# The RWKV scan of a four-layer network: the factors of the inverse applied one by one, products laid crosswise

## The reference

```python
def step(S, inp):
    rt, wt, kt, vt, kkt, bt = inp
    sk = jnp.einsum('bhij,bhj->bhi', S, kkt)
    S = S * wt[:, :, None, :] - sk[..., None] * bt[:, :, None, :] + vt[..., None] * kt[:, :, None, :]
    return S, jnp.einsum('bhij,bhj->bhi', S, rt)
S, ys = lax.scan(step, S0, xs, reverse=reverse)
```

## Time and profile before

| | us |
|---|---|
| median of three runs (2982.25 to 2987.36) | 2986.35 |
| the profiled execution | 2984.68 |
| its span in the trace | 2982.9 |
| PE busy | 2852.2 |
| DVE busy | 2072.6 |
| ACT busy | 604.3 |
| POOL busy | 306.7 |

### The profile page before, as it was taken

The page is one execution under the profiler, slowest core; times in us unless marked ns, Lnnn a source line. Parts: engine busy times, 40 slices in busy tenths (PEclk is TensorE's granted clock), DMA queues, the critical chain, the costliest instruction groups (busy, mean ns, idle before and its releaser), DMA issues.

```text
span 2982.9 us, 62866 instructions
## 1 busy us (share of the span) xinstructions
PE 2852.2 (96%) x27428; PEld 2641.3 (89%) x27428; DVE 2072.6 (69%) x3617; ACT 604.3 (20%) x1385; POOL 306.7 (10%) x518
## 2 busy tenths in 40 slices
PE   7999998889989999999999999989999999999998
PEld 6888886777887999999899999977889999977998
DVE  6777636555564798997869889836249989853864
ACT  2000004343332200201320021024121021022201
POOL 0001002432341001001000100000000100000000
PEclk8999999999999999999999999999999999999999
DMA  7556413003103688687347868733457868823452
GB/s 282 169 177 233 139 46 110 3 4 113 46 4 127 204 269 279 214 280 241 99 159 259 298 205 268 239 108 117 138 181 249 297 206 260 278 75 99 142 191 92
DMA packets 387504, 514.54 MB, mean 172 GB/s; under 512 B 14032, under 2 KB 344976, under 8 KB 386080
## 3 DMA queue, kind: packets, MB, share of 16 engines
q1 hardware_dynamic: 347632, 366.73, 37.9%
q0 software_dynamic: 39456, 143.67, 14.0%
q10 hardware_dynamic: 144, 0.13, 0.0%
HBM read 509.44 MB, written 1.05 MB: 171 GB/s over the span
## 4 chain that ended last, share of the span: by engine, by line
PE 87%; DVE 5%; ACT 3%; DMA 2%; issue 2%; POOL 1%; SPq 0%; DVEq 0%; ACTq 0%; POOLq 0%
PE PS L2580 39%; PE PS L2640 20%; PE PS L662 6%; PE PS L682 5%; PE PS L839 3%; PE PS L1754 2%; PE PS L1679 2%; PE PS L2652 1%; PE PS L1530 1%; PE PS L2500 1%; PE PS L1436 1%; PE PS L698 1%; PE PS L2518 1%; DMA W<-in_ffn_in 1%; DMA W<-in_e_w_in 0%
## 5 line engine op out<-in xcount | busy, mean ns | idle before, releaser
L2580 PE MATMUL PS<-X,W 128*128 128x128 f32 x3360 | 411.9, 276 | 6.2 <-ACT JUNK L2763 3.3
L2580 PEld LDWEIGHTS PS<-X,W 128*128 128x128 f32 x3360 | 393.2, 192 | 7.9 <-ACT JUNK L2763 4.8
L2640 PE MATMUL PS<-ARENA,W 128*128 128x128 f32 (+1 forms) x2816 | 362.3, 288 | 2.6 <-DVE ARENA L2943 1.6
L2640 PEld LDWEIGHTS PS<-ARENA,W 128*128 128x128 f32 x2816 | 346.3, 192 | 12.6 <-DVE ARENA L2943 2.0
L2867 DVE SCALAR_TENSOR_TENSOR ADAW<-ADAW,CB 128x1024 f32<-128x1024 f32 x280 | 332.4, 1218 | 0.6
L2471 POOL DMA_DIRECT2D ADAW<-in_ada_rows x272 | 144.4, 532 | 1820.8 <-DVE ADAW L2867 1476.4
L2580 PE MATMUL PS<-Y,W 128*128 128x128 f32 (+2 forms) x2096 | 311.8, 302 | 2.8 <-DVE Y L3178 1.8
L2580 PEld LDWEIGHTS PS<-Y,W 128*128 128x128 f32 x2096 | 285.2, 192 | 18.6 <-issue 1.8
L2580 PE MATMUL PS<-Y,ARENA 128*128 128x128 f32 (+2 forms) x1632 | 217.1, 286 | 2.2 <-DVE ARENA L2928 2.2
L2580 PEld LDWEIGHTS PS<-Y,ARENA 128*128 128x128 f32 x1632 | 203.1, 191 | 7.5 <-DVE ARENA L2928 3.0
L2914 DVE TENSOR_TENSOR ARENA<-W 128x1024 f32<-128x1024 f32 (+1 forms) x120 | 159.3, 1327 | 16.7 <-DMA W<-in_ffn_in 5.7
(11 more groups left out here) (470 smaller groups left out, 4313.2 us busy)
## 6 DMA issues: line engine op xcount, KB each, us to landing
...
```

Of the source, the lines that this page charges most:

```text
L2580: last = mm(block_bank(b, q, half), w[left][:, k, q * P:(q + 1) * P], yb[right][:, k], start=(k == 0 and p not in (2, 5)), stop=(k == 3), ...
L2640: last = mm(block_bank(b, 0, half), w[left][:, k], hb[right][:, k], start=(k == 0 and p not in (2, 5)), stop=(k == PAIRS - 1), skip_group_ ...
```

## The change

The inverse is no longer put together. DD and the factors (F, F2, F4 of MO x DD) are applied to the right side one by one: DG = DD x GG, then F4I, F2I and FI (U1, U2, UU). GG comes in two parts, GS from the state (copied by ACT) and GV from the values, added on DVE. The values have one form, VT1, UU0 and VT0 are gone. Scores, masks and most lists are laid out crosswise, by direction; N2 and M2 stay straight, and so do GV and, in the latent scan, YS, a part of the output that is made early and added to it by DVE. POOL makes BH for both halves first, then KH. The masks have half the columns; the constant "scores" stands in for one in a later layer. Lines without a sign and most removed lines are left out below.

```diff
     eye = np.eye(HD, dtype=bool)
     blk = (i[:, None] // 8) == (i[None, :] // 8)
     for name, sign, pick in (("strict", 1.0, lambda u: u), ("incl", 1.0, lambda u: u | eye), ("nincl", -1.0, lambda u: u | eye),
-                             ("nblk", -1.0, lambda u: u & blk), ("noff", -1.0, lambda u: u & ~blk),
+                             ("nblk", -1.0, lambda u: u & blk), ("moff", -1.0, lambda u: u.T & ~blk),
                              ("mblk", -1.0, lambda u: u.T & blk)):
-        both = np.concatenate([pick(u) for u in up], 1)
-        add(name, np.concatenate([both, both], 0) * sign)
+        add(name, np.concatenate([pick(u) for u in up], 0) * sign)
+    add("scores", np.concatenate([up[0] | eye] * 2, 0) * 1.0)
     add("eye64", np.concatenate([np.eye(HD)] * 2, 0))
...
-        MD, ND, NO, IMD, M4I, N2I, ET2I = [unit(7 + i) for i in range(7)]
-        TI, GG, UU0, UU1, KHT, BHT, VT0, VT1, AK, ARK = [unit(14 + i) for i in range(10)]
+        MD, ND, MO, IMD, N2, N2I, F2I = [unit(7 + i) for i in range(7)]
+        M4, GG, UU1, KHT, BHT, VT1, AK, ARK, GS_ = [unit(14 + i) for i in range(9)]
-        N2, M2, P1M = M4I, ND, MD
-        M4, DD, DTR, EE, ETR, ETI, EE2, ET2, ET4I, Q1, Q2 = TI, M4I, ND, MD, IMD, N2I, ND, NO, MD, IMD, ND
+        M2, P1M = ND, MD
+        DD, FF_, FT_, FI, F2, FT2, F4I, DG, U1, U2 = ND, MD, IMD, N2I, N2, MO, MD, M4, IMD, N2
...
+        PE_EV = ["N2", "M2", "M4", "P1", "DD", "AKK", "F", "FT", "F2", "FT2", "F4", "VT", "KHT", "GS", "GV", "KBT", "DG", "U1",
+                 "U2", "UU"]
+        PE_LAT = PE_EV[:-2] + ["YS"] + PE_EV[-2:]
+        DVE_EV = ["N2", "N2I", "M4I", "AK", "F", "F2", "F4I", "GG", "BHT", "U1"]
...
+            def one_bank(t, g, left, right):
+
+                for q in range(TQ * t, TQ * (t + 1)):
+                    for f in range(2):
+                        c = slice(q * P + f * HD, q * P + (f + 1) * HD)
+                        o = (q % TQ) * P + f * HD
+                        for h in range(2):
+                            y = right(h, f, q) if callable(right) else right[half(h), c]
+                            last = mm(bank(t, 1, g)[half(h), o:o + HD], left[half(h), c], y, start=True, stop=True)
+                return last
+
...
-                                last = mm(bank(t, s, d)[half(g), o:o + P], left[half(g), c:c + HD], kr4(n)[half(g), q, :, d],
+                                last = mm(bank(t, s, g)[half(d), o:o + P], left[half(g), c:c + HD], kr4(n)[half(g), q, :, d],
-                                last = mm(bank(t, s, d)[half(g), o:o + HD], left[half(g), c:c + HD],
+                                last = mm(bank(t, s, g)[half(d), o:o + HD], left[half(g), c:c + HD],
-                pe.wait_ge(s_po[t], e_pool.after(n, "KBH"))
+                pe.wait_ge(s_po[t], e_pool.after(n, "BH"))
-                            o = (q % TQ) * P + d * HD
-                            last = mm(bank(t, 1)[half(g), o:o + HD], kr4(n)[half(g), q, 0, d], BH[half(g), c:c + HD],
+                            o = (q % TQ) * HD
+                            last = mm(bank(t, 1, g)[half(d), o:o + HD], kr4(n)[half(g), q, 0, d], BH[half(g), c:c + HD],
...
+                    products(t, 0, (MD, ND, False)).then_inc(s_pp[t], 1)
+                    products(t, 1, (ND, MD, False)).then_inc(s_pp[t], 1)
+                    products(t, 1, (N2, M2, True)).then_inc(s_pp[t], 1)
+                    products(t, 0, (IMD, N2I, True)).then_inc(s_pp[t], 1)
+                    products(t, 1, (M4, P1M, True)).then_inc(s_pp[t], 1)
+                    pe.wait_ge(s_po[t], e_pool.after(n, "KH"))
+                    beside(t, 0, KH, n).then_inc(s_pp[t], 1)
+                    products(t, 1, (MO, DD, True)).then_inc(s_pp[t], 1)
+                    products(t, 0, (DD, MO, True)).then_inc(s_pp[t], 1)
+                for t in range(NT):
+                    pe.wait_ge(s_vd[t], e_dve.after(n, "F"))
+                    pe.wait_ge(s_va[t], e_act.after(n, "FT"))
+                    products(t, 1, (FT_, FF_, True)).then_inc(s_pp[t], 1)
+                    products(t, 0, (FF_, FT_, True)).then_inc(s_pp[t], 1)
+                for t in range(NT):
+                    pe.wait_ge(s_vd[t], e_dve.after(n, "F2"))
+                    pe.wait_ge(s_va[t], e_act.after(n, "FT2"))
+                    products(t, 0, (FT2, F2, True)).then_inc(s_pp[t], 1)
+                    turned(t, 1, 1, KH).then_inc(s_pp[t], 1)
+                for t in range(NT):
+                    pe.wait_ge(s_vd[t], e_dve.after(n, "F4I"))
+                    pe.wait_ge(s_va[t], e_act.after(n, "VT1"))
+                    products(t, 0, (keys(n, 0), MST, True)).then_inc(s_pp[t], 1)
+                    one_bank(t, 0, AK, VT1).then_inc(s_pp[t], 1)
+                    pe.wait_ge(s_va[t], e_act.after(n, "KHT"))
+                    turned(t, 1, 1, BH).then_inc(s_pp[t], 1)
+                for t in range(NT):
+                    pe.wait_ge(s_vd[t], e_dve.after(n, "GG"))
+                    products(t, 0, (DD, GG, True)).then_inc(s_pp[t], 1)
+                for t in range(NT):
+                    pe.wait_ge(s_va[t], e_act.after(n, "DG"))
+                    products(t, 0, (F4I, DG, True)).then_inc(s_pp[t], 1)
+                    if lat:
+                        one_bank(t, 0, MST, keys(n, 1)).then_inc(s_pp[t], 1)
+                for t in range(NT):
+                    pe.wait_ge(s_vd[t], e_dve.after(n, "U1"))
+                    pe.wait_ge(s_po[t], e_pool.after(n, "F2I"))
+                    products(t, 0, (F2I, U1, True)).then_inc(s_pp[t], 1)
+                        pe.wait_ge(s_vd[t], e_dve.after(n, "YS" if lat else "BHT"))
+                    pe.wait_ge(s_vd[t], e_dve.after(n, "U2"))
+                    products(t, 0, (FI, U2, True)).then_inc(s_pp[t], 1)
+                    pe.wait_ge(s_vd[t], e_dve.after(n, "BHT"))
+                    products(t, 1, (KHT, VT1, True), (BHT, UU1, True)).then_inc(s_pp[t], 1)
+                        products(t, 0, (VT1, ARK, True), (UU1, ARB[n % 2], True))\
+                            .then_inc(s_pp[t], 1)
...
+                    exps(0, n + 1)
+                for t in range(NT):
+                    act.wait_ge(s_pp[t], e_pe.after(n, "FT"))
+                    out(FT_, t, 0).then_inc(s_va[t], 1)
+                if more:
+                    exps(1, n + 1)
+                for t in range(NT):
+                    act.wait_ge(s_pp[t], e_pe.after(n, "FT2"))
+                    out(FT2, t, 0).then_inc(s_va[t], 1)
+                for t in range(NT):
+                    A(part(VT1, t), flat(t, 1, 0), ACT.Copy).then_inc(s_va[t], 1)
+                    act.wait_ge(s_pp[t], e_pe.after(n, "KHT"))
+                    A(part(KHT, t), flat(t, 1, 1), ACT.Copy).then_inc(s_va[t], 1)
+                if more:
+                    inverse_exps(0, n + 1)
+                for t in range(NT):
+                    act.wait_ge(s_pp[t], e_pe.after(n, "GS"))
+                    out(GS_, t, 0).then_inc(s_va[t], 1)
+                if more:
+                    inverse_exps(1, n + 1)
+                for t in range(NT):
+                    act.wait_ge(s_pp[t], e_pe.after(n, "DG"))
+                    out(DG, t, 0).then_inc(s_va[t], 1)
...
+            def masked(dst, t, which, name, s):
+                return V.tensor_tensor(cols4(dst)[:, qs(t)], outs_beside(t, s)[:, :, :, which], mask(name), ALU.mult)
+                of = outs(t, 1)
+                V.tensor_tensor(cols4(MO)[:, qs(t)], of, mask("moff"), ALU.mult)
+                    masked(ARB[n % 2], t, 1, "nincl", 1)
+                masked(ND, t, 0, "nblk", 1).then_inc(s_vf[t], 1)
...
+                        masked(ARK, t, 1, "incl", 0)
+                    masked(AK, t, 0, "strict", 0).then_inc(s_vd[t], 1)
...
+                    dve.wait_ge(s_pp[t], e_pe.after(n, "F4"))
+                    dve.wait_ge(s_po[t], e_pool.after(n, "FI"))
+                    out_and_eye(F4I, t, 0).then_inc(s_vd[t], 1)
+                for t in range(NT):
+                    dve.wait_ge(s_pp[t], e_pe.after(n, "GV"))
+                    dve.wait_ge(s_va[t], e_act.after(n, "GS"))
+                    V.tensor_tensor(part(GG, t), flat(t, 1, 0), part(GS_, t), ALU.add).then_inc(s_vd[t], 1)
+                for t in range(NT):
+                    dve.wait_ge(s_pp[t], e_pe.after(n, "KBT"))
+                    V.tensor_scalar(part(BHT, t), flat(t, 1, 1), -1.0, None, ALU.mult).then_inc(s_vd[t], 1)
...
+                for t in range(NT):
+                    dve.wait_ge(s_pp[t], e_pe.after(n, "U1"))
+                    out(U1, t, 0).then_inc(s_vd[t], 1)
+                    if lat:
+                        dve.wait_ge(s_pp[t], e_pe.after(n, "YS"))
+                        of = flat(t, 1, 0).rearrange("p (q f e) -> p q f e", q=TQ, f=2)
+                        for f in range(2):
+                            c = n % CH if f == 0 else CH - 1 - n % CH
+                            y = YO[:, qs(t), c * HD:(c + 1) * HD]
```

(21 more changed lines are left out.)

125 lines of the change are left out of this document (21 added, 104 removed).

## The result

The changed kernel takes 2968.72 us (median of seven runs, 2963.10 to 2975.74) against 2986.35 for the kernel before (seven runs, 2981.50 to 2989.41): a ratio of 0.9947 [0.9932, 0.9961]. The forecast was 2969.5. Timed again twice beside other kernels it gave 0.9952 and 0.9949. The profiled execution took 2971.60 us with a span of 2969.7, 13.2 less than before.

A forecast was written before the change was run, and what follows sets the result against it. The prediction took instruction packets fetched for PE to bound the two scans. From the profiled 2984.7 us: -11.9 packets, 0 crossing, -4 hand-overs, -1 start gives 2967.8, or 2969.5 us as a median; its own range was 2961 to 2983.

The forecast's parts named there:

- What bounds the scan: In both RWKV scans PE executes a 16 KB packet of some 250 instructions, then waits for the next; 3.88 us each.
- The forecast's sign of it: In the scans' profile after: PE busy less, "issue" the same or more, a packet still 3.6 to 3.9 us.
- packets had come closer together than 3.4 us: Sign against the forecast, on the scans' instruction queue: closer packets would mean the fetch was not the bound.
- the first rival: In the scans PE's own time counts, so crossing's 38 us arrive: 2948 us; chance 6%.
- Packets, -11.9: In both scans, one list fewer per half and chunk: 768 instructions, 3.07 packets at 3.88 us, 11.9 us less.
- Crossing, 0: Scans' straight lists (0.70 us) becoming crossed (0.36) save 38 us of PE's time, all turned into "issue": counted as nothing.
- The reason for the 0.70 us: Straight lists in the scans put both row halves into one PSUM bank one after the other; crossed ones alternate banks.
- Hand-overs, -4: Late hand-overs between engines in the scans fall from 16 to 12 us; range -12 to +8.
- three chunks run about 3 us over: Three latent chunks with bonus terms: VectorE's queue of 12.8 us against PE's 2.7 packets, 9.8 us; 9 us in all.
- The last sign: The forecast is wrong if a latent-scan chunk without bonus terms is as long as one with them.
- The start, -1: At the first scan's start BH1 is ready 2.4 us earlier, but VectorE writes MO and MD first: -1 (0 to -2).
- The fourth rival: Crossing idles the array and both scans run at the 1.2 GHz clock: +68 us, 3037 us; chance 5%.

The follow-up runs named there:

- The three lists put back: Changed kernel with its F list issued four times in a row, 2304 instructions more: 2997.69 us, 1.0057 of the kernel before.
- BH first: Kernel before with GpSimd's part of the change alone, BH of both halves made first, then KH: 2979.89 us, 0.9989 of the kernel before.
- with the number of instructions of before: Changed kernel with its F list issued twice, 768 instructions more, as many as the kernel before: 2976.81 us, 0.9989 of the kernel before.

## Why the prediction was right

*What bounds the scan.* Right. The forecast's sign of it, busy time down and "issue" up at an unchanged packet price, is in the profile: 253.4/68 = 3.73 us a packet against 275.2/71 = 3.88, with 258 instructions to each in both. (The prediction's 250 counted its windows alone; 768/258 is 3.0 packets as well.) The three lists put back brought more time back than PE's own. The prediction would have been wrong if packets had come closer together than 3.4 us. The nearest two in the changed kernel's scans start 3.25 us apart, but in the kernel before 3.36, and 3.26 with BH first: the 3.4, read from slices of 0.375 us, was too coarse, and the median distance hardly moved, 3.7 us where it was 3.8 to 3.9. The Trainium skill (Runtime: NRT & Kernel Launch, "Instruction fetch mechanics") has the fetch mostly hidden; it is not hidden here, and the first rival, which hung on it, did not come.

*Packets, -11.9.* Three fewer, as counted; at 3.73 us they are -11.2.

*Crossing, 0.* Right only in the main. In the two windows PE's busy time fell by 39 us, the windows by 21 us, of which 11 are packets. Its zero may have been too strict: with the number of instructions of before, the new order is 3.3 us faster (0 to 7) and 9.5 us by the scans. How much of that is crossing, how much hand-overs and how much the tiles' addresses isn't separated. The reason for the 0.70 us, taken from the Trainium skill (TensorEngine Tiling (Array Packing), "Gotcha 1: PSUM Pressure"), was wrong for this kernel: straight lists take 0.70 us with one bank and with a new bank at each product. The sum did not use it.

*Hand-overs, -4.* This was the term that was mis-sized. The pair of profiles has -21.8 in the scans, of which -11.2 are packets: -10.6 is left for this term and whatever crossing and addresses gave. By the means (271.6 and 253.8) it is -17.8, and -6.6 is left. The step that failed is "three chunks run about 3 us over": PE waited behind the bonus terms 3.0, 1.1 and 1.0 us, and taking that away was worth 0.8 us a chunk, since PE then stood for the packet. VectorE's queue was summed with nearly the right lengths (GG to the last mask of the next chunk took 10.8 us in the middle chunk, forecast 12.8, since the small sums and copies overlap), but the packet against which it was set comes late anyhow. The last sign, a latent chunk without bonus terms as long as one with them, can't be read: the only such chunk is the last (31.4 us against 34.2 to 35.7), and it has no next chunk's products either.

*The start, -1.* The cause was right and the size too small. From the first product to the end of the first list it takes 7.5 us in the kernel before, 4.9 with POOL's order alone and 4.7 to 5.5 in four profiles of the new scan. The table's -2.2 agrees by chance, since the first product itself starts up to 2 us earlier or later in three profiles of the changed kernel (536.9 to 539.0). POOL's wait is gone; PE now waits for VectorE's masks, 1.47 and 0.35 us:

```profile
539.30 0.58 PE L713 MATMUL PS<-W 64*64 64x64 f32 x24 [1.47 <-DVE W L1096]
540.23 0.87 PE L713 MATMUL PS<-W 64*64 64x64 f32 x24 [0.35 <-DVE W L1096]
```

*What the prediction did not have.* Behind the scan 9.3 us were given back in the pair, 8.5 in the means, and 1.5 between the scans in the pair. The pair adds up to -11.2 - 10.6 - 2.2 + 1.5 + 9.3 = -13.2 us, where the forecast had -16.9 and the medians have -17.6, which no profile takes apart. So that the forecast of 2969.5 is met by 0.8 us is luck: a gain in the scans larger than forecast and a loss behind them that it did not have nearly cancel. The fourth rival had the clock in the scans, where it hardly fell (0.99 in both windows); it fell elsewhere and cost some 5 us, not 68. The range of the forecast itself is 2960 to 2984 us by its own terms; it says 2961 to 2983.
